# GpSimd in place of VectorE for the sums of the down weights' half slabs, two units ahead

## The chip, the cores and the metric

One core of a Trainium2 chip runs the whole program in one launch. The metric is the device time of that core in microseconds, the median of several executions; lower is better. A core has five instruction engines that run side by side and meet through semaphores: TensorE (PE; its weight loads are listed as PEld), VectorE (DVE), ScalarE (ACT), GpSimd (POOL) and SyncE (SP), which here only issues DMAs. ScalarE issues DMAs too.

## What is computed

A transformer-like trunk of two layers over 1088 tokens in fp32. Each layer is a mixer (sparse attention and a short convolution) and then a squared-ReLU MLP; the change lies in the last product of the MLP, `w_down`, 4096 x 1024 per layer:

```python
def trunk_layer(x, ..., w_up, w_down, topk):
    a, k_new, v_new, ki_new, conv_new = token_mixers(rms_norm(x, gains[0]), ...)
    x = x + rms_norm(a, gains[1])
    f = jnp.square(jax.nn.relu(rms_norm(x, gains[2]) @ w_up)) @ w_down
    x = x + rms_norm(f, gains[3])
    return x, k_new, v_new, ki_new, conv_new
```

## The kernel before

Every fp32 operand of a product is held as two fp32r numbers, a high part and a rest (value minus high part), and a product is three matmuls: high x high, high x rest, rest x high.

**The down projection by seven products.** The first 1024 rows of `w_down` are multiplied plainly, at the end (L778). The other 3072 rows are cut in two halves, and so are the 1024 output columns and the tokens, which gives 2x2 blocks; a scheme of Strassen's kind makes the product from seven block products ("forms", counted q = 0 to 6 in the order of `POSF = [0, 3, 1, 4, 2, 5, 6]`). A form has four pairs of output tiles, each in two **units**: eight units per form, `NUNIT` = 56 per layer, n = 8q + j. A unit is a half slab of weights, 128x768, six row blocks by 128 columns; TensorE makes 36 matmuls from it (`down_unit`, L1238).

**How a unit's weights come.** SyncE loads the half slab into `DR[n % 4]` (L567; buffers named DR or RAW in the profile), and for forms 1 and 3 a second one into `SK[n % 8]` (L566). For the units in `SUMMED` (forms 1, 3, 4 and 5; 32 per layer) the weights of the form are a sum or difference of two half slabs: `unit_add` on VectorE writes it into SK or DR (L2701, L2703). ScalarE then copies the high part into `DW[n % 4]` (`unit_high`; its copies are all on L1311), after TensorE has finished unit n - 4, and GpSimd makes the rest (L731). When GpSimd has made the rest of unit n (`unit_lo`), SyncE may load unit n + 4 into the buffer. TensorE waits for `unit_lo` before each unit.

**How a form's activations come.** ScalarE loads twelve blocks of 128x536 (128x528 in the second layer) of the next form into FL in three DMAs of 1.07 MB (L1832), copies their high parts into FB, and VectorE makes the rests (`form_low`, L2710), three at each of j = 4 to 7. TensorE waits for the first six before unit 0 of the form and for all twelve before unit 1. The products of a pair are added from PSUM to X by VectorE (`quads_out`, L2737, one to three instructions; L2739 copies for form 0), in the same in-order queue, behind the rests:

```python
for n in range(NUNIT):                      # VectorE
    q, j = divmod(n, 8)
    if n + 4 in SUMMED:
        unit_add(n + 4)
    if j >= 4:
        if q + 1 < len(POSF):
            form_low(q + 1, range(3 * (j - 4), 3 * (j - 3)))
    ...
    if j % 2:
        quads_out(q, j // 2)
```

Every engine works its list in the order in which it is written; nothing else sets the order. GpSimd's list in this stage is the 56 rests (L728 to L731), between the forms of the up weights (L695 to L716) and the splits of the plain down slabs (L600, L602).

Of the kernel before, what the change touches and what calls it, by code (L numbers as in the profile page):

```python
# [21 lines left out]
ALU, ACT, AX = mybir.AluOpType, mybir.ActivationFunctionType, mybir.AxisListType  # L22
# [67 lines left out]
POSF = [0, 3, 1, 4, 2, 5, 6]  # L90
NUNIT = len(POSF) * DPAIRS * 2
# [6 lines left out]
SUMMED = [n for n in range(NUNIT) if POSF[n // 8] in (2, 3, 4, 5)]  # L98
# [36 lines left out]
def key_tiles(t):  # L135

    if t == SPECIAL:
        return [(0, SEQ, MS, SPECIAL), (MS, PAST0, PAST, SPECIAL + 1)]
    return [(N_META + P * j, P * j, P, j) for j in range(t + 1)] + [(0, META0, N_META, SPECIAL)]
# [65 lines left out]
def build(nc, d):  # L205
    ctx = ExitStack()
    with ctx:
        names = set()

        def sem(name):  # L210
            assert name not in names
            names.add(name)
            return ctx.enter_context(nc.semaphore(name))
# [16 lines left out]
        def at(name, shape, dt, offset):  # L230
            return nc.alloc_sbuf_tensor_at(name, shape, dt, offset=offset)
# [66 lines left out]
        def prob(PA, i, g):  # L298
# [55 lines left out]
        DR = [RAW[:, 0, 0:UCOLS], RAW[:, 1, 0:UCOLS], at("DR2", [P, UCOLS], F32, r_q + 2 * ROW)[:, :],  # L354
              at("DR3", [P, UCOLS], F32, r_w + 4 * UCOLS * 4)[:, :]]
# [100 lines left out]
        unit_in = [sem("unit_in%d" % i) for i in range(4)]  # L456
        unit_sum, unit_hi, unit_lo, unit_done = sem("unit_sum"), sem("unit_hi"), sem("unit_lo"), sem("unit_done")
# [28 lines left out]
        def unit_loads(l, n):  # L486

            f, s = POSF[n // 8], n % 4
            before = sum(1 + (POSF[m // 8] in KEPT_OF) for m in range(n % 4, NUNIT, 4))
            return (l * before + sum(1 + (POSF[m // 8] in KEPT_OF) for m in range(s, n + 1, 4))) * 16  # L490

        def unit_value(l, n):

            return AREA[l][UNIT_SK][n % 8][:, :] if POSF[n // 8] in (2, 3, 4) else DR[n % 4]

        def sums_to(l, n):

            return l * len(SUMMED) + SUMMED.index(n) + 1
# [4 lines left out]
        def rows_at(u):  # L503

            a, kv, kt = STEPS[u]
            n = len(key_tiles(ORDER[a]))
            return [(j, g) for j, g in ROW_UNITS if j == NKV * a + kv + 2 and min(max(g, 0), n - 1) == kt]


        ENDS = [u + 1 for u, (_, _, kt) in enumerate(STEPS) if u + 1 == NU or STEPS[u + 1][2] == 0]  # L510

        def raw_q(l, k):
# [80 lines left out]
        def _(g_):  # L593
# [30 lines left out]
            for l in range(DEPTH):  # L624
# [63 lines left out]
                def forms(g, first=False):  # L688

                    n = l * NSTR + g  # L690
                    i = (l * (NRAW // 2) + KT // 2 + (S_UP + NPLAIN) // 2 + g + 1) * 16

                    def lo(f, value, done):
                        g_.wait_ge(form_hi, n * NPROD + f + 1)
                        g_.tensor_tensor(WF[f][:, 1, :, :], value, WF[f][:, 0, :, :].bitcast(F32), ALU.subtract)\  # L695
                          .then_inc(done, 1)

                    g_.wait_ge(raw_in[0], i)
                    g_.wait_ge(raw_in[1], i)
                    g_.tensor_tensor(S1F[:, :, :], a21, a22, ALU.add).then_inc(sum_made, 1)  # L700
                    lo(0, a11, form_made)
                    g_.wait_ge(sum_made, n * 4 + 1)
                    if first:
                        g_.wait_ge(slab_done, l * NDONE + D_MLP + NPLAIN)
                    else:
                        g_.wait_ge(prod_done, (n - 1) * NPROD + 3)
                    g_.tensor_tensor(WS[2][:, 1, :, :], S1F[:, :, :], a11, ALU.subtract).then_inc(sum_made, 1)
                    g_.wait_ge(sum_made, n * 4 + 2)
                    if first:
                        g_.wait_ge(t_step, l * 16 + 12)  # L710
                        g_.wait_ge(mid_stored, (l + 1) * NCH * 16)
                    g_.tensor_tensor(S4F[:, :, :], a12, WS[2][:, 1, :, :], ALU.subtract).then_inc(sum_made, 1)
                    lo(1, a12, form_made)
                    if not first:
                        g_.wait_ge(prod_done, (n - 1) * NPROD + 4)
                    g_.tensor_tensor(WS[3][:, 1, :, :], a21, a11, ALU.subtract).then_inc(sum_made, 1)  # L716
                    g_.wait_ge(sum_made, n * 4 + 3)
                    lo(2, WS[2][:, 1, :, :], form_made)
                    g_.wait_ge(sum_made, n * 4 + 4)
                    lo(3, WS[3][:, 1, :, :], raw_split)  # L720
                    lo(4, S1F[:, :, :], form_made)
                    lo(5, S4F[:, :, :], form_made)
                    lo(6, a22, raw_split)

                forms(0, True)
                with g_.Fori(1, NSTR) as g:
                    forms(g)
                for n in range(NUNIT):  # L728
                    hi, lo = (DW[n % 4][:, w, :, :].rearrange("p k n -> p (k n)") for w in range(2))
                    g_.wait_ge(unit_hi, l * NUNIT + n + 1)  # L730
                    g_.tensor_tensor(lo, unit_value(l, n), hi.bitcast(F32), ALU.subtract).then_inc(unit_lo, 1)  # L731
# [1299 lines left out]
        def _(dve):  # L2031
            V_ = nc.vector
# [129 lines left out]
            for l in range(DEPTH):  # L2162
# [215 lines left out]
                for b in range(BITS - 1, -1, -1):  # L2378
# [7 lines left out]
                    n = BITS - 1 - b  # L2386
# [107 lines left out]
                for u, (a, kv, kt) in enumerate(STEPS):  # L2494
                    i, n, rows = NKV * a + kv, len(key_tiles(ORDER[a])), rows_at(u)
# [19 lines left out]
                with dve.Fori(0, NMERGE // 2) as g:  # L2515
                    for s in range(2):
                        n = l * NMERGE + g * 2 + s
# [172 lines left out]
                products_out(NSTR - 1, False, True)  # L2690
                t_sums(NSTR - 1, 0, 4)

                def unit_add(n):

                    f, kept, raw_ = POSF[n // 8], SK[n % 8][:, :], DR[n % 4]
                    dve.wait_ge(unit_in[n % 4], unit_loads(l, n))
                    if f in (2, 5):
                        dve.wait_ge(unit_lo, l * NUNIT + n - 7)
                        dve.wait_ge(unit_sum, sums_to(l, n) - 8)
                    if f == 5:  # L2700
                        last = V_.tensor_tensor(raw_, raw_, kept, ALU.subtract)  # L2701
                    else:
                        last = V_.tensor_tensor(kept, kept, raw_, ALU.add if f == 4 else ALU.subtract)  # L2703
                    last.then_inc(unit_sum, 1)

                def form_low(q, kks):

                    for kk in kks:
                        dve.wait_ge(f_hi, (l * 7 + q) * NFORM + kk + 1)
                        V_.tensor_tensor(FB[q % 2][:, 1, kk, 0:2 * QWL[l]], FL[q % 2][:, kk, 0:2 * QWL[l]],  # L2710
                                         FB[q % 2][:, 0, kk, 0:2 * QWL[l]].bitcast(F32), ALU.subtract).then_inc(f_lo, 1)

                def a_low(j):

                    dve.wait_ge(a_hi, l * NPA + j + 1)
                    if j == 0 and TL[l] > 4 * QWL[l]:
                        V_.memset(A[:, :, :, 4 * QWL[l]:TL[l]].bitcast(F32), 0.0)
                    V_.tensor_tensor(A[:, 1, j, 0:4 * QWL[l]], ALO[:, j, 0:4 * QWL[l]],
                                     A[:, 0, j, 0:4 * QWL[l]].bitcast(F32), ALU.subtract).then_inc(a_lo, 1)
# [21 lines left out]

                for n in range(NUNIT):
                    q, j = divmod(n, 8)
                    if n + 4 in SUMMED:
                        unit_add(n + 4)
                    if j >= 4:
                        if q + 1 < len(POSF):
                            form_low(q + 1, range(3 * (j - 4), 3 * (j - 3)))
                        else:
                            a_low(2 * (j - 4))  # L2750
                            a_low(2 * (j - 4) + 1)
                    if j % 2:
                        quads_out(q, j // 2)
# [147 lines left out]
```

## Time and profile before

| | us |
|---|---|
| median of 3 runs | 3215.02 (3215.01 to 3217.68) |
| profiled execution, its own time | 3214.36 |
| its span, first to last instruction | 3212.4 |
| TensorE busy | 3070.5 (96%) |
| VectorE busy | 2170.1 (68%) |
| GpSimd busy | 1244.4 (39%) |
| ScalarE busy | 1064.3 (33%) |

Times in the trace count from the first instruction of the span. The seven products run from 1260 to 1518 us in the first layer and from 2842 to 3097 us in the second. A group of instructions is named by its line, engine and operation, then output tile <- input tiles. What stands in brackets at the end of a row of the timeline is how long the engine was idle before it and what released it.

### The profile page before, as it was taken

To read this page: it belongs to the slowest core of one execution; us is meant where nothing else is said; L and a number is where in the kernel's file an instruction comes from. 1 tells how busy PE (TensorE), PEld (TensorE's weight loads), DVE (VectorE), ACT (ScalarE), POOL (GpSimd) and SP (SyncE) were. 2 spreads that over 40 slices of the span, in tenths; PEclk is the share of its full clock that TensorE was granted. 3 is DMA by queue.
4 is the path that set the end of the run, shared out by engine and by line. 5 is a ranking of instruction groups with operands and counts; after the bars stand their busy time and mean duration, and the time that the engine had idled before them with its cause. 6 is when DMAs were issued, how large, how long until landed. Compare 5 with 4: busy or idle time off the path is not lost.

```text
span 3212.4 us, 54404 instructions
## 1 busy us (share of the span) xinstructions
PE 3070.5 (96%) x20484; PEld 2941.8 (92%) x20484; DVE 2170.1 (68%) x3821; ACT 1064.3 (33%) x1938; POOL 1244.4 (39%) x733
## 2 busy tenths in 40 slices
PE   5999999999999999999979999989999899999997
PEld 4989998679999999999979899977799899999997
DVE  6269998945585555675482799988456855576735
ACT  5430112750353333333244201137313433333321
POOL 2023333004637665445330333320154476644460
PEclk8999998999999999999999999989999999999998
DMA  3121223103323446654331212230132334466433
GB/s 136 54 72 46 68 87 134 34 28 128 115 82 121 146 136 214 238 191 171 99 120 60 67 47 80 91 115 27 67 107 96 109 127 147 147 247 241 170 127 108
DMA packets 164542, 369.50 MB, mean 115 GB/s; under 512 B 18496, under 2 KB 60064, under 8 KB 164384
## 3 DMA queue, kind: packets, MB, share of 16 engines
q10 hardware_dynamic: 114112, 209.45, 18.1%
q1 hardware_dynamic: 50272, 157.96, 15.2%
q8 instruction: 97, 1.59, 0.2%
q14 instruction: 61, 0.50, 0.0%
HBM read 261.53 MB, written 105.83 MB: 114 GB/s over the span
## 4 chain that ended last, share of the span: by engine, by line
PE 80%; DVE 10%; DMA 3%; issue 2%; ACT 2%; POOL 1%; ACTq 1%; DVEq 0%; SPq 0%; POOLq 0%
PE PS L769 26%; PE PS L1173 17%; PE PS L1238 13%; PE PS L778 8%; PE PS L852 5%; PE PS L1071 3%; PE PS L1031 2%; PE PS L1054 2%; PE PS L940 1%; PE PS L902 1%; PE PS L884 1%; DVE FB L2710 1%; DVE X L2139 1%; DVE X L2145 1%; DVE HN L2094 1%
## 5 line engine op out<-in xcount | busy, mean ns | idle before, releaser
L769 PE MATMUL PS<-H,W 128*128 128x358 f32 (+1 forms) x4032 | 662.0, 326 | 3.2 <-ACT SQ L1735 3.2
L769 PEld LDWEIGHTS PS<-H,W 128*128 128x128 f32 x4032 | 660.7, 189 | 3.3 <-issue 3.3
L600 POOL TENSOR_TENSOR W<-RAW,ones 128x1024 fp32r<-128x1024 f32 x80 | 157.4, 1967 | 880.6 <-PE PS L769 828.4
L1238 PE MATMUL PS<-FB,DW 128*128 128x268 f32 (+1 forms) x3456 | 428.1, 287 | 9.5 <-DVE FB L2710 9.5
L1238 PEld LDWEIGHTS PS<-FB,DW 128*128 128x128 f32 x3456 | 427.5, 190 | 9.8 <-POOL DW L731 9.8
L2363 DVE TENSOR_SCALAR_CACHE_REDUCE PASS<-SC,TC,CST 128x400 bf16<-128x400 f32 x372 | 356.1, 1020 | 1.7
L1173 PE MATMUL PS<-TT,WF 128*128 128x268 f32 (+1 forms) x2688 | 339.1, 285 | 0.8 <-POOL WF L695 0.8
L1173 PEld LDWEIGHTS PS<-TT,WF 128*128 128x128 f32 x2688 | 333.8, 188 | 1.0 <-POOL WF L695 1.0
L1173 PE MATMUL PS<-H,WF 128*128 128x268 f32 (+1 forms) x2016 | 260.2, 287 | 4.9 <-POOL WF L695 4.9
L1173 PEld LDWEIGHTS PS<-H,WF 128*128 128x128 f32 x2016 | 254.2, 190 | 5.3 <-POOL WF L695 5.3
L852 PE MATMUL PS<-WQ,H 128*128 128x364 f32 (+1 forms) x1296 | 239.9, 341 | 12.1 <-POOL WQ L607 5.5
L852 PEld LDWEIGHTS PS<-WQ,H 128*128 128x128 f32 (+1 forms) x1296 | 215.6, 187 | 21.6 <-ACT H L1311 8.9
L602 POOL TENSOR_TENSOR W<-RAW,W 128x1024 fp32r<-128x1024 f32 x80 | 211.4, 2642 | 6.3
L769 PE MATMUL PS<-A,W 128*128 128x358 f32 (+1 forms) x1152 | 188.7, 326 | 0.0
L769 PEld LDWEIGHTS PS<-A,W 128*128 128x128 f32 x1152 | 188.1, 189 | 0.6 <-issue 0.6
L778 PE MATMUL PS<-H,WR 128*128 128x358 f32 (+1 forms) x1008 | 167.1, 326 | 0.0
L778 PE MATMUL PS<-A,WD 128*128 128x358 f32 (+1 forms) x1008 | 166.9, 326 | 0.0
L778 PEld LDWEIGHTS PS<-A,WD 128*128 128x128 f32 x1008 | 164.0, 188 | 0.0
L778 PEld LDWEIGHTS PS<-H,WR 128*128 128x128 f32 x1008 | 163.6, 188 | 0.0
L1071 PE MATMUL PS<-PT,V 128*128 128x512 f32 (+2 forms) x304 | 157.6, 601 | 1.6 <-ACT PT L1311 1.6
L1031 PE MATMUL PS<-KS,QS 128*128 128x512 f32 (+6 forms) x480 | 134.9, 400 | 19.9 <-DVE LEAST L2427 17.1
L2737 DVE TENSOR_TENSOR X<-X,PS 128x536 f32<-128x536 f32 (+1 forms) x80 | 53.7, 703 | 147.1 <-PE PS L1238 147.1
(254 smaller groups left out, 4957.9 us busy)
## 6 DMA issues: line engine op xcount, KB each, us to landing
RAW<-in_w_slab SPq DMA_DIRECT2D x168, 512.0 KB, 3.6
RAW<-in_w_half SPq DMA_DIRECT2D x56, 384.0 KB, 4.3
DR<-in_w_half SPq DMA_DIRECT2D x56, 384.0 KB, 3.6
FL<-f_keep ACTq DMA_DIRECT2D x18, 1072.0 KB, 10.3
FL<-f_keep ACTq DMA_DIRECT2D x18, 1056.0 KB, 9.5
f_keep<-TB ACTq DMA_DIRECT2D x48, 268.0 KB, 4.5
f_keep<-TB ACTq DMA_DIRECT2D x48, 264.0 KB, 4.4
SK<-in_w_half SPq DMA_DIRECT2D x32, 384.0 KB, 3.8
```

The source lines that it names most:

```text
L600: g_.tensor_tensor(hi, raw, one, ALU.mult).then_inc(hi_split, 1)
L602: g_.tensor_tensor(lo, raw, hi.bitcast(F32), ALU.subtract).then_inc(raw_split, 1)
L769: mm = nc.tensor.matmul(PS[:, b0 + c, 0:cw], W[:, s, w, k, :], act[:, a, k, c * cw:(c + 1) * cw], start=(first and w == 0 and a == 0), sto ...
L778: mm = nc.tensor.matmul(PS[:, bank_, 0:cw], w[:, h, k, :], act[:, a, k, c * cw:(c + 1) * cw], start=(k == first and h == 0 and a == 0), st ...
L852: return nc.tensor.matmul(PS[0:m, b, 0:QG], H[:, a, k, t * P:t * P + m], WQ[:, k, w, b * QG:(b + 1) * QG], start=(k == 0 and w == 0 and a ...
L1031: last = nc.tensor.matmul(flat[0:m, c0 + dst:c0 + dst + w], QS[:, a % 3, GROUP * kv + q, 0:m], KS[:, 2 * kv + x, key:key + w], start=(x == ...
L1054: last = nc.tensor.transpose(PS[0:w, 4 + u % 2, g * m:(g + 1) * m], prob(PA, i, g)[0:m, dst:dst + w], cst["ident"][0:m, 0:m])
L1071: nc.tensor.matmul(PS[:, 6 + kv, 0:GROUP * m], V[0:w, vt, :], PT[0:w, u % 3, 0:GROUP * m], start=(kt == 0), stop=(kt == len(key_tiles(t)) ...
L1173: last = nc.tensor.matmul(PS[:, 2 * (f % 4) + c, 0:qw], WF[f][:, w, k, :], act(a, k, c * qw, (c + 1) * qw), start=(k == 0 and w == 0 and a ...
L1238: last = nc.tensor.matmul(PS[:, to + c, 0:qw], DW[s][:, w, kk - u * UNITK, :], down_act(q, a, kk, c * qw, (c + 1) * qw), start=(kk == 0 an ...
L2363: did(V_.tensor_scalar(PASS[0:m, SC_OFF[t]:SC_OFF[t] + EXT[t]], row(t), at_least, cst["negk"][0:m, c:c + 1], op, ALU.add, accum_out=CNT[0: ...
L2737: last = V_.tensor_tensor(to, to, of, ALU.add)
```

## The change

`unit_add` moves from VectorE to GpSimd, word for word but for the engine that issues it. On VectorE it ran at step n for unit n + 4; on GpSimd it runs at step n for unit n + 2, ahead of the rest of unit n. Its waits stay: for the loads of its unit (`unit_in`), and in forms 4 and 5 for the rest of the unit eight before it and the add eight before it. ScalarE, TensorE and SyncE wait for the same semaphores as before.

```diff
@@ GpSimd
                 with g_.Fori(1, NSTR) as g:
                     forms(g)
+                def unit_add(n):
+
+                    f, kept, raw_ = POSF[n // 8], SK[n % 8][:, :], DR[n % 4]
+                    g_.wait_ge(unit_in[n % 4], unit_loads(l, n))
+                    if f in (2, 5):
+                        g_.wait_ge(unit_lo, l * NUNIT + n - 7)
+                        g_.wait_ge(unit_sum, sums_to(l, n) - 8)
+                    if f == 5:
+                        last = g_.tensor_tensor(raw_, raw_, kept, ALU.subtract)
+                    else:
+                        last = g_.tensor_tensor(kept, kept, raw_, ALU.add if f == 4 else ALU.subtract)
+                    last.then_inc(unit_sum, 1)
+
                 for n in range(NUNIT):
+                    if n + 2 in SUMMED:
+                        unit_add(n + 2)
                     hi, lo = (DW[n % 4][:, w, :, :].rearrange("p k n -> p (k n)") for w in range(2))
                     g_.wait_ge(unit_hi, l * NUNIT + n + 1)
                     g_.tensor_tensor(lo, unit_value(l, n), hi.bitcast(F32), ALU.subtract).then_inc(unit_lo, 1)
@@ VectorE
-                def unit_add(n):
...
                 for n in range(NUNIT):
                     q, j = divmod(n, 8)
-                    if n + 4 in SUMMED:
-                        unit_add(n + 4)
                     if j >= 4:
```

GpSimd in the first layer, from the rest of unit 4 to that of unit 9. DW is where the rest goes, SK and DR or RAW are the half slabs. Before:

```order
L731 TENSOR_TENSOR DW_149<-RAW,DW_149 128x768
L731 TENSOR_TENSOR DW_150<-RAW,DW_150 128x768
L731 TENSOR_TENSOR DW_151<-DR_176,DW_151 128x768
L731 TENSOR_TENSOR DW_152<-DR_177,DW_152 128x768
L731 TENSOR_TENSOR DW_149<-SK_0_81,DW_149 128x768
L731 TENSOR_TENSOR DW_150<-SK_0_82,DW_150 128x768
```

The same place on GpSimd in the changed kernel, where L738 is the add and L746 the rest:

```order
L746 TENSOR_TENSOR DW_149<-RAW,DW_149 128x768
L746 TENSOR_TENSOR DW_150<-RAW,DW_150 128x768
L738 TENSOR_TENSOR SK_0_81<-SK_0_81,RAW 128x768
L746 TENSOR_TENSOR DW_151<-DR_176,DW_151 128x768
L738 TENSOR_TENSOR SK_0_82<-SK_0_82,RAW 128x768
L746 TENSOR_TENSOR DW_152<-DR_177,DW_152 128x768
L738 TENSOR_TENSOR SK_0_83<-SK_0_83,DR_176 128x768
L746 TENSOR_TENSOR DW_149<-SK_0_81,DW_149 128x768
L738 TENSOR_TENSOR SK_0_84<-SK_0_84,DR_177 128x768
L746 TENSOR_TENSOR DW_150<-SK_0_82,DW_150 128x768
```

The adds of units 8 and 9 now stand ahead of the rests of units 6 and 7, and so on, one add before each rest.

VectorE in the first layer, second half of form 2, where it makes the rests of form 3 (FB) between the X adds. Before:

```order
L2703 TENSOR_TENSOR SK_0_81<-SK_0_81,RAW 128x768
L2710 TENSOR_TENSOR FB_0_78<-FL_0_80,FB_0_78 128x536 x3
L2703 TENSOR_TENSOR SK_0_82<-SK_0_82,RAW 128x768
L2710 TENSOR_TENSOR FB_0_78<-FL_0_80,FB_0_78 128x536 x3
L2737 TENSOR_TENSOR X<-X,PS 128x536
L2703 TENSOR_TENSOR SK_0_83<-SK_0_83,DR_176 128x768
L2710 TENSOR_TENSOR FB_0_78<-FL_0_80,FB_0_78 128x536 x3
L2703 TENSOR_TENSOR SK_0_84<-SK_0_84,DR_177 128x768
L2710 TENSOR_TENSOR FB_0_78<-FL_0_80,FB_0_78 128x536 x3
```

The same place on VectorE in the changed kernel (L2712 the rests, L2739 the X adds):

```order
L2712 TENSOR_TENSOR FB_0_78<-FL_0_80,FB_0_78 128x536 x6
L2739 TENSOR_TENSOR X<-X,PS 128x536
L2712 TENSOR_TENSOR FB_0_78<-FL_0_80,FB_0_78 128x536 x6
```

The four adds are gone from between the rests; rests and X adds keep their order.

## Rows read from the trace of the kernel before

**Rows 1.** The page: the chain that ended last, by engine.
```profile
PE 80%; DVE 10%; DMA 3%; issue 2%; ACT 2%; POOL 1%; ACTq 1%; DVEq 0%; SPq 0%; POOLq 0%
```

**Rows 2.** Chain of waits, start us, us, what: first layer, then second.
```profile
1278.84 8.21 DMA RAW<-in_w_half
...
1287.07 0.96 DVE SK L2703
...
2868.78 0.96 DVE SK L2703
```

**Rows 3.** Stretches, engines' busy time; third number from the end: granted clock of TensorE.
```profile
1309.00:1311.00 2.00, 2.00 (x11) 2.00 (x10) 2.00 (x4) 0.40 (x1) 0.00 (x0) 0.50 1.05 419
2889.00:2891.00 2.00, 2.00 (x9) 2.00 (x10) 2.00 (x4) 0.00 (x0) 0.00 (x0) 0.50 1.04 395
1264.60:1266.10 1.50, 0.07 (x2) 0.04 (x1) 1.50 (x4) 0.84 (x1) 0.58 (x1) 1.00 1.02 405
```

**Rows 4.** Timeline of TensorE, cut at 1320 and at 2900 us.
```profile
1266.09 31.52 PE L1238 MATMUL PS<-H,DW 128*128 128x268 f32 x252 [1.44 <-DVE H L2623]
1307.36 12.80 PE L1238 MATMUL PS<-FB,DW 128*128 128x268 f32 x85 [5.29 <-DVE FB L2710]
...
2880.25 4.55 PE L1238 MATMUL PS<-FB,DW 128*128 128x264 f32 x36
2888.96 11.25 PE L1238 MATMUL PS<-FB,DW 128*128 128x264 f32 x78 [4.16 <-DVE FB L2710]
```

**Rows 5.** Groups (min/median/max ns), the half slabs' loads, VectorE's rests (mean ns last).
```profile
L2703 DVE TENSOR_TENSOR SK<-SK,RAW x12: 941/946/2393, 1287.1 to 1415.5; 128x768 f32<-128x768 f32 x12
...
L700 POOL TENSOR_TENSOR S1F<-RAW x28: 1283/1292/1301, 947.2 to 2807.2; 128x512 f32<-128x512 f32 x28
...
DMA to landing us min/median/max: 2.8/3.8/8.8
...
L2710 DVE TENSOR_TENSOR FB<-FL,FB 128x536 fp32r<-128x536 f32 x72 | 72.7, 1066 | 0.0
```

**Rows 6.** Timelines: GpSimd's rests near form 1, VectorE's copies; the long rest.
```profile
1276.60 3.65 POOL L731 TENSOR_TENSOR DW<-RAW,DW 128x768 fp32r<-128x768 f32 x2 [2.65 <-ACT DW L1311]
1280.21 1.85 POOL L731 TENSOR_TENSOR DW<-DR,DW 128x768 fp32r<-128x768 f32 x1
1288.99 1.99 POOL L731 TENSOR_TENSOR DW<-SK,DW 128x768 fp32r<-128x768 f32 x1 [4.38 <-ACT DW L1311]
...
1279.78 2.58 DVE L2739 COPY X<-PS 128x536 f32<-128x536 f32 x4 [3.17 <-PE PS L1238]
...
1443.99 4.70 POOL L731 TENSOR_TENSOR DW<-DR,DW 128x768 fp32r<-128x768 f32 x1 [2.62 <-ACT DW L1311]
```

**Rows 7.** Timeline of form 3, first layer: TensorE's releases, rests, X adds.
```profile
1394.12 1.34 DVE L2737 TENSOR_TENSOR X<-X,PS 128x536 f32<-128x536 f32 x2 [4.39 <-PE PS L1238]
1395.11 1.85 POOL L731 TENSOR_TENSOR DW<-SK,DW 128x768 fp32r<-128x768 f32 x1 [2.59 <-ACT DW L1311]
1398.63 0.85 ACT L1311 ACTIVATE DW<-SK 128x768 fp32r<-128x768 f32 x1 [1.98 <-PE PS L1238]
1403.98 1.32 DVE L2737 TENSOR_TENSOR X<-X,PS 128x536 f32<-128x536 f32 x2
1403.99 1.86 POOL L731 TENSOR_TENSOR DW<-SK,DW 128x768 fp32r<-128x768 f32 x1 [1.76 <-ACT DW L1311]
1409.33 3.61 DVE L2710 TENSOR_TENSOR FB<-FL,FB 128x536 fp32r<-128x536 f32 x3
1416.40 0.85 ACT L1311 ACTIVATE DW<-SK 128x768 fp32r<-128x768 f32 x1 [3.60 <-PE PS L1238]
1429.67 1.96 DVE L2737 TENSOR_TENSOR X<-X,PS 128x536 f32<-128x536 f32 x3 [4.38 <-PE PS L1238]
```

**Rows 8.** Timeline before the up projection, where VectorE and GpSimd both have work queued.
```profile
964.78 5.87 DVE L2576 TENSOR_TENSOR TT<-TF,TT 128x536 fp32r<-128x536 f32 x4
...
970.04 1.74 POOL L716 TENSOR_TENSOR WS<-RAW 128x512 f32<-128x512 f32 x1
```

More of the change, by code:

```diff
@@ L2691, in _ @@
                 t_sums(NSTR - 1, 0, 4)
-                def unit_add(n):
[L2695 to L2704, printed above, removed]
                 def form_low(q, kks):
```

## The prediction

> **What bounds the kernel now.** I read the page first. TensorE is busy for 96% of the span and is 80% of the chain that ended last [rows 1], so what only keeps it fed costs nothing. The down products (L1238) are one of its stretches: 3456 + 576 matmuls, and in them it waited in three places only: 5.3 us and 4.2 us for VectorE's rest of a form (FB, L2710), one per layer, and once 1.4 us [rows 4]. Between these waits it is the bound, and VectorE and GpSimd only have to be in time.
>
> The chain of waits says what the 5.3 us are made of [rows 2]: a half slab lands at 1287.07, and from there until TensorE goes on at 1307.36 VectorE alone is the path: add, three rests, add, three rests, copies, add, three rests, add, three rests. The adds are what the change takes off. After the wait TensorE runs at a granted clock of 0.50 (1.2 GHz) for a while [rows 3]: 85 matmuls take 12.80 us, where 252 take 31.52 (0.125 each, so 85 should take 10.6) [rows 4]. The stall costs 5.3 + 2.2 = 7.5 us; in the second layer 78 matmuls take 11.25 instead of 9.6, so 4.2 + 1.6 = 5.8 us. The 1.4 us wait left the clock at 1.00 [rows 3]. **13.3 us is all that can be won.**
>
> **What the change removes.** 64 adds of 128x768 from VectorE, 0.95 us each alone [rows 5]. Except at the two places above none is on the path.
>
> **What it adds.** The same 64 on GpSimd. The trace has no 128x768 add there, but it has the same form with 512 columns (1.29 us), and GpSimd's rest of 768 columns takes 1.85, or 3.65 for two in a row [rows 5, 6]. Adding and subtracting two SBUF tensors is one shape, so I take 1.83 in a row; the cheapest it could be is 1.29, the dearest 1.99. GpSimd then has 3.65 us in each unit of weights. A unit of TensorE is (1429.67 - 1394.12)/8 = 4.44 us, by VectorE's adds of the same pair in forms 3 and 4 [rows 7]. By itself that fits, with 0.8 us to spare.
>
> **What does not fit: the two engines exclude each other.** In the rows before 970 VectorE's TT rests and GpSimd's operations take turns, strictly one to one: four rests take 5.87 us, of which the first is free (0.70) and the others 1.72 each, and a GpSimd operation of 512 columns 1.74 in place of 1.29 [rows 8]. A turn of 1.72 holds 1.29 of GpSimd's, so each VectorE operation on two SBUF tensors costs GpSimd 0.43 us, and each GpSimd operation holds back one VectorE operation for all its length. Sums with a PSUM operand don't take part: two X adds took 1.32 us beside a GpSimd rest of 1.86 [rows 7]. With both queued, one pair takes 1.82 + 0.43 = 2.25 us, and GpSimd's two operations per unit make 4.5 us: just TensorE's pace of 4.44. GpSimd is then never idle long enough for a second VectorE operation, and **VectorE gets two rests per unit.** It needs twelve for each form.
>
> Now the deadline. VectorE's rests of form q+1 start after the X adds of pair 1 of form q (unit 4 begins) and the last six are wanted when unit 1 of form q+1 begins: five units, 22.2 us. In form 3 of the first layer: adds at 1394.12, last rest ended at 1409.33 + 3.61 = 1412.94, TensorE passed that point at 1416.40 (ScalarE's release for the unit three further on) [rows 7]. Slack 3.5 us, already with four adds and five waits for GpSimd in between.
>
> After the change, walked from these rows: the first rest is asked for at 1395.4, GpSimd's rest of 1395.11 is busy until 1396.96 [rows 7], so it ends at 1397.5. Then one per GpSimd operation, 2.25 us apart: add, rest, add, rest. Once, near 1399.6, GpSimd's rest has to wait for its high part (ScalarE starts that only when TensorE releases the buffer, at 1398.63 [rows 7]) and a second VectorE rest slips in for 0.7. The X adds in the middle (1.3 us) fall into one GpSimd operation. Last rest: 1397.5 + 0.7 + 10 x 2.25 = 1420.7. **TensorE waits 4.3 us.** While it waits GpSimd stops too, its buffers being full, but only two or three of its operations later. In form 2 (one X add per pair in place of two) the same walk gives 4.0 us, in form 4 (three) 4.5. Forms 1, 5 and 6 make their successors' rests when GpSimd has no adds to make: unchanged. In the second layer TensorE's unit is 0.05 us shorter, so 0.25 more each. Sum 2 x 12.8 + 0.75 = **26.4 us**. Waits of 5.3 and 4.2 us both brought the clock down for 2.2 and 1.6 us [rows 3, 4]; six times 2.0 is **12 us** (bounds: nothing, if the clock holds as after 1.4 us, and 13).
>
> **The start of form 1.** On GpSimd the add for unit 8 now stands ahead of the rest of unit 6 (listing in the section on the change), and it waits for the half slab that lands at 1287.07 (2868.8 in the second layer). The rest of unit 6 was made at 1280.21 [rows 6]; now add and rest end at 1290.8. TensorE wants it at 1266.09 + 5 x 4.50 = 1288.6 [rows 4]: a new wait of 2.3 us; in the second layer 2872.5 against 2880.25 - 2 x 4.39 = 2871.5, some 1.2. Queued behind it are the loads for units 10 and 11, which SyncE issues on the rests of 6 and 7; each lands some 4 us later (median 3.8 [rows 5]), when TensorE is at unit 8. VectorE instead makes its first six rests from 1282.4 on [rows 6], before any GpSimd add. The other six take turns with GpSimd, whose adds wait for loads: they end at 1293.2, 1295.5, 1297.8, 1300.0, 1302.3 and 1304.6, where TensorE, 2.3 us late, wants the last at 1304.4. So 7.5 becomes 2.6, and 5.8 becomes 1.7: 9.0 us won. Bounds: all of the 13.3; or nothing, if the clock also falls at the new wait and units 10 to 15, whose loads share the queue with 3.3 MB of forms and then took 8.2 us to land [rows 2], make TensorE wait 1 to 3 us more. I take **7 us** won.
>
> **Sum.** 26.4 + 12 - 7 = +31, which counts every pair as a loss. One slip of the turns is on record: VectorE made an add and three rests in a row while a GpSimd rest took 4.7 us [rows 6], and each such slip saves 2.2 us of a stall, or the stall's clock. I take 4 us off for them: +27 us on the profiled 3214.4, 3241.4. That run stands 0.7 under the median of 3215.0, so **3242 us**.
>
> **A rule of the Trainium skill.** The trace shows a VectorE operation costing GpSimd 0.43 us where it lasts 0.63 to 0.70 [rows 8]. The Trainium skill (SBUF — State Buffer, section "SBUF: two separate sides") calls the shared ports "an **exclusive lock**, not a bandwidth split", held for the whole instruction. The trace agrees on the exclusion but not on the whole length. By the page this change would end later than I say, so it is a rival.
>
> **Rivals.**
> (a) The turns cost full length. A pair is 1.84 + 0.70 = 2.54 us; the ten pairs of a walk add 10 x 0.29 = 2.9 us to each of six stalls, +17: 3259. Against it: four pairs at 1.72 in [rows 8].
> (b) GpSimd becomes the bound by its chain: rest n frees a buffer, the load takes 3.8 to 8.4 us, then add n+4, then rest. Two units per chain: 3.8 + 1.85 + 1.85 = 7.5 us against 8.9 is in time; with 8.4 us it is 12.1, 3.2 late, three or four times a layer where the forms' loads run. Its reserve of three units (13 us) covers that except at form 1. Some +20 on the forecast if the reserve is gone: 3262.
> (c) The starving is half as bad: one or two slips in each walk, stalls of 2.1 us, clock untouched: 6 x 2.1 - 7 = +6, 3221. The slip above speaks for it; in the other rows GpSimd gave way once at most.
> (d) The other side: VectorE is in time. It loses four adds (0.95 to 2.4 us each, 5.7 us in the walk of form 3 [rows 7]) against 3.5 us of slack that it has already; if GpSimd's added operations hold it back less than 9.2 us in a walk, no new stall appears, and the start of form 1 gives 9 to 13: 3205. It decides at about five extra waits of 1.8 us, and I count six or seven.
> (e) Nothing moves, because what is won at form 1 is lost in unit 6 and small stalls: with (c).
>
> **How the numbers follow.** Forecast 0.62 (3226 to 3258), (a) 0.10, (b) 0.08, (c, e) 0.10, (d) 0.10. The range from 3214 to 3262 leaves out (d) and the far part of (a) and (b). Within 0.2% (what a measurement can tell, 6.4 us) means 3208.6 to 3221.4: (c, e), 0.10; faster (d), 0.10; slower 0.80.
>
> **What would show it.** TensorE's waits in the down products: beside unit 6, waits of about 4 us for FB's rest at unit 1 of forms 3, 4 and 5, six in all, each followed by a clock of 0.50; VectorE's rests with a mean well over the 1.07 us of now [rows 5]; GpSimd's adds at 1.9 to 2.3 us. I am wrong if VectorE's rests for a form end before TensorE starts its unit 1, if GpSimd yields more than one turn at a time as a rule, or if TensorE's waits name GpSimd's DW.

## The result and the profile after

The changed kernel takes 3256.62 us (median of 4 runs, 3254.38 to 3261.48) against 3216.35 for the kernel before (3215.01 to 3221.0): ratio 1.0123, 95% interval 1.0111 to 1.0135. It is **40 us slower**; forecast were 27. The profiled execution is the slowest of the four (3261.48 us), so its trace has some 5 us more than the median.

The page of the changed kernel, busy time and the chain that ended last. GpSimd has 64 operations and 133 us more; VectorE has 64 fewer and no less busy time, because busy time counts what an instruction waits for its turn beside GpSimd (a rest of a form lasts 2.31 us in the median, where it lasted 0.70).

```profile
PE 3095.2 (95%) x20484; PEld 2963.3 (91%) x20484; DVE 2172.6 (67%) x3757; ACT 1064.2 (33%) x1938; POOL 1377.5 (42%) x797
...
PE 75%; DVE 13%; DMA 4%; issue 3%; ACT 2%; POOL 2%; ACTq 1%; SPq 0%; DVEq 0%; POOLq 0%
```

TensorE's waits in the changed kernel, 1240 to 1560 us, then 2850 to 3150 (total, times, longest). They answer to the waits in [rows 4].

```profile
PE PS L1253 <- DVE FB L2712: 14.2, 3, 5.7
PE PS L1253 <- POOL DW L746: 4.0, 3, 2.8
...
PE PS L1253 <- DVE FB L2712: 14.1, 4, 5.1
PE PS L1253 <- POOL DW L746: 4.0, 2, 2.2
```

The timeline of TensorE in the seven products of the first layer shows where they lie. The block that starts at 1299.70 is unit 8; 1316.45 is unit 11; 1384.08, 1427.12 and 1470.44 are unit 1 of forms 3, 4 and 5.

```profile
1265.48 24.10 PE L1253 MATMUL PS<-H,DW 128*128 128x268 f32 x180 [1.79 <-DVE H L2638]
1290.65 9.21 PE L1253 MATMUL PS<-H,DW 128*128 128x268 f32 x72 [1.06 <-POOL DW L746]
1299.70 4.62 PE L1253 MATMUL PS<-FB,DW 128*128 128x268 f32 x36
1304.53 9.17 PE L1253 MATMUL PS<-FB,DW 128*128 128x268 f32 x72 [0.21 <-POOL DW L746]
1316.45 64.01 PE L1253 MATMUL PS<-FB,DW 128*128 128x268 f32 x504 [2.76 <-POOL DW L746]
1384.08 37.31 PE L1253 MATMUL PS<-FB,DW 128*128 128x268 f32 x288 [3.62 <-DVE FB L2712]
1427.12 38.43 PE L1253 MATMUL PS<-FB,DW 128*128 128x268 f32 x288 [5.73 <-DVE FB L2712]
1470.44 68.43 PE L1253 MATMUL PS<-FB,DW 128*128 128x268 f32 x540 [4.88 <-DVE FB L2712]
```

In the second layer the same places wait for 1.79 (unit 6), 2.17 (unit 11), 3.86, 4.93 and 5.11 us. Behind each wait of over 2 us the granted clock is at half for a while, here in two-microsecond stretches after the waits at 1427 and 1470 (third number from the end); these answer to [rows 3].

```profile
1428.00:1430.00 2.00, 2.00 (x11) 2.00 (x11) 0.22 (x1) 0.00 (x0) 1.79 (x1) 0.50 1.05 403
1471.00:1473.00 2.00, 2.00 (x11) 2.00 (x11) 1.16 (x2) 0.00 (x0) 1.04 (x1) 0.50 1.05 398
```

The mechanism itself, in form 3 of the first layer, VectorE and then GpSimd. It answers to [rows 7]; L746 is the rest, L738 the sum.

```profile
1399.21 1.34 DVE L2739 TENSOR_TENSOR X<-X,PS 128x536 f32<-128x536 f32 x2 [7.56 <-PE PS L1253]
...
1414.58 12.39 DVE L2712 TENSOR_TENSOR FB<-FL,FB 128x536 fp32r<-128x536 f32 x6
1426.90 1.32 DVE L2739 TENSOR_TENSOR X<-X,PS 128x536 f32<-128x536 f32 x2
...
1415.09 2.31 POOL L746 TENSOR_TENSOR DW<-SK,DW 128x768 fp32r<-128x768 f32 x1
1417.36 2.31 POOL L738 TENSOR_TENSOR SK<-SK,RAW 128x768 f32<-128x768 f32 x1
1419.64 2.30 POOL L746 TENSOR_TENSOR DW<-SK,DW 128x768 fp32r<-128x768 f32 x1
1421.90 2.27 POOL L738 TENSOR_TENSOR SK<-SK,DR 128x768 f32<-128x768 f32 x1
```

What VectorE and GpSimd hold in turns, one operation at a time, is called the port from here on. GpSimd's operations start 2.28 us apart, 0.45 us more than the 1.83 that the same operation lasts alone, and six rests of VectorE take 12.39 us where 6 x 0.63 = 3.8 would do. The twelfth rest ends at 1414.58 + 12.39 = 1426.97; TensorE had finished unit 0 of form 4 at 1384.08 + 37.31 = 1421.39.

### The profile page after: what moved, and what is told of

Same layout as the page of the kernel before. It is cut to its first block, busy times and chain, and to the rows that moved or that the text cites. A ratio compares the mean times of both kernels' runs of the same rounds, so it can differ in the third digit from the quotient of the medians.

```text
span 3259.6 us, 54404 instructions
## 1 busy us (share of the span) xinstructions
PE 3095.2 (95%) x20484; PEld 2963.3 (91%) x20484; DVE 2172.6 (67%) x3757; ACT 1064.2 (33%) x1938; POOL 1377.5 (42%) x797
## 4 chain that ended last, share of the span: by engine, by line
PE 75%; DVE 13%; DMA 4%; issue 3%; ACT 2%; POOL 2%; ACTq 1%; SPq 0%; DVEq 0%; POOLq 0%
PE PS L784 26%; PE PS L1188 16%; PE PS L1253 9%; PE PS L793 8%; PE PS L867 5%; DVE FB L2712 4%; PE PS L1086 3%; PE PS L1046 2%; PE PS L1069 2%; PE PS L955 1%; PE PS L917 1%; DMA RAW<-in_w_half 1%; PE PS L899 1%; DVE X L2154 1%; DVE X L2160 1%
## 5 line engine op out<-in xcount | busy, mean ns | idle before, releaser
L1253 PE MATMUL PS<-FB,DW 128*128 128x268 f32 (+1 forms) x3456 | 442.5, 292 | 33.5 <-DVE FB L2712 28.3
L1253 PEld LDWEIGHTS PS<-FB,DW 128*128 128x128 f32 x3456 | 440.3, 195 | 35.4 <-issue 23.7
L2712 DVE TENSOR_TENSOR FB<-FL,FB 128x536 fp32r<-128x536 f32 (+1 forms) x144 | 231.8, 1674 | 0.0
L2739 DVE TENSOR_TENSOR X<-X,PS 128x536 f32<-128x536 f32 (+1 forms) x80 | 53.6, 702 | 184.4 <-PE PS L1253 184.4
```

The costliest lines, as they stand in the source:

```text
L1253: last = nc.tensor.matmul(PS[:, to + c, 0:qw], DW[s][:, w, kk - u * UNITK, :], down_act(q, a, kk, c * qw, (c + 1) * qw), start=(kk == 0 an ...
```

## The experiments

My theory was the forecast's: the rests of VectorE starve beside two GpSimd operations per unit. Rivals were that GpSimd's own chain is late, that the start of form 1 spoils what follows, and that it is the amount of work and not the taking of turns.

**1. Form 1 alone.** GpSimd makes the sums of form 1 only; the last two lines of the diff are VectorE's.

```diff
-                    if n + 2 in SUMMED:
+                    if n + 2 in SUMMED and (n + 2) // 8 in (1,):
                         unit_add(n + 2)
...
+                    if n + 4 in SUMMED and (n + 4) // 8 not in (1,):
+                        unit_add(n + 4)
```

> GpSimd makes only the sums of form 1 (units 8 to 15); those of forms 3, 4 and 5 are back on VectorE, four units ahead, as before the change. Theory (VectorE's rests starve because each has to take its turn behind one of two GpSimd operations per unit): no waits of 3.6 to 5.7 us at unit 1 of forms 3, 4, 5; the start of form 1 as in the changed kernel, waits of 1.1 and 2.8 us in the first layer, 1.8 and 2.2 in the second, in place of 5.3 and 4.2, so 0 to 6 us faster than before: 3211 to 3216. Rival (GpSimd's own chain of load, sum and rest is late, and VectorE's rests are only late because of it): about half of the loss stays, 3230 or more.

Measured: 3216.36 us, ratio 1.000 (0.9991 to 1.001). No form after the first makes TensorE wait for rests; what is left, by TensorE's waits in both layers, lies at the start of the products:

```profile
PE PS L1253 <- POOL DW L746: 6.1, 4, 2.5
PE PS L1253 <- DVE H L2638: 4.0, 3, 1.8
PE PS L1253 <- DVE X L2754: 2.7, 1, 2.7
```

So the start of form 1, where I had counted on 7 us, gains nothing that can be measured: waits for VectorE (5.3 and 4.2 us) have become waits for GpSimd, and once 2.7 us for a copy of products to X. The low clock is not gone either: it was 0.53 and 0.50 behind two of GpSimd's waits, of 2.3 and 2.5 us.

**2. Forms 3, 4 and 5 alone.** The same edit with `(3, 4, 5)` in place of `(1,)`.

> The other half alone: GpSimd makes the sums of forms 3, 4 and 5, VectorE those of form 1. Theory: all six waits for VectorE's rests stay at 3.6 to 5.7 us (28 in all) with some 12 us of low clock behind them, and the start of form 1 is as before with 5.3 and 4.2: 38 to 44 us slower than before. Rival (the loss comes out of form 1, which leaves GpSimd without reserve for the forms that follow): under 15 us slower.

Measured: 3257.67 us (one run), as slow as the whole change. TensorE's waits for VectorE's rests (eight: the two at form 1 and the six) are all there:

```profile
PE PS L1253 <- DVE FB L2725: 34.9, 8, 5.1
PE PS L1253 <- DVE H L2638: 3.6, 2, 1.8
```

The whole loss is in forms 3, 4 and 5, and form 1 has no part in it.

**3. Half as long.** The changed kernel with sums of half the columns; the kernel leaves out the other half, so its output is another.

```diff
-                        last = g_.tensor_tensor(raw_, raw_, kept, ALU.subtract)
+                        last = g_.tensor_tensor(raw_[:, 0:UCOLS // 2], raw_[:, 0:UCOLS // 2], kept[:, 0:UCOLS // 2], ALU.subtract)
```

(and the other line likewise).

> The changed kernel with sums over 384 of 768 columns; half of each sum is left out. As many turns as in the changed kernel, but every second one is about 0.9 us shorter. Theory: the mean turn falls from 2.28 to 1.83 us, twelve rests end 5 us earlier, and the six waits for them shrink from 3.6 to 5.7 us to under 1.5 us each: 3210 to 3222. Rival (what counts is that there are two waits for GpSimd per unit, semaphores and all, not their length): waits over 3 us stay, 3245 or more.

Measured: 3207.86 us (one run). TensorE waits for no rest of VectorE any more; in both layers together there are three waits for GpSimd of 2.2 us in all. The number of GpSimd's operations does no harm; their time on the port does. The time is even below the range that I gave, since at form 1 TensorE then waits 2.2 us in place of 9.5, with no low clock behind it: the two layers' products take 9.9 us less than in the kernel before, of the 13.3 that there were to win.

**4. Longer rests.** The changed kernel, VectorE's rests three blocks at a time.

```diff
-                    for kk in kks:
-                        dve.wait_ge(f_hi, (l * 7 + q) * NFORM + kk + 1)
-                        V_.tensor_tensor(FB[q % 2][:, 1, kk, 0:2 * QWL[l]], FL[q % 2][:, kk, 0:2 * QWL[l]],
-                                         FB[q % 2][:, 0, kk, 0:2 * QWL[l]].bitcast(F32), ALU.subtract).then_inc(f_lo, 1)
+                    k0, k1 = kks.start, kks.stop
+                    dve.wait_ge(f_hi, (l * 7 + q) * NFORM + k1)
+                    V_.tensor_tensor(FB[q % 2][:, 1, k0:k1, 0:2 * QWL[l]], FL[q % 2][:, k0:k1, 0:2 * QWL[l]],
+                                     FB[q % 2][:, 0, k0:k1, 0:2 * QWL[l]].bitcast(F32), ALU.subtract).then_inc(f_lo, k1 - k0)
```

> The changed kernel, but VectorE makes the rests of a form three blocks at a time: 4 instructions of 128x1608 in place of 12 of 128x536, the same elements. Theory (turns, not elements, are short): 4 turns of at most 1.85 + 1.7 us, so no wait for a form's rests; waits at units 6 and 11 stay; 3205 to 3215, faster than before. Rival (the shared port is simply full, 37 us of work in 35.6 us per form): the work is the same, so waits of 2 us and more stay, or GpSimd is late in its place: 3235 or more.

Measured: 3241.13 us, ratio 1.0078 (1.0061 to 1.0095). Half right on both sides: the waits for VectorE are gone, as the theory said, but GpSimd is late in its place, 31 times, as the rival said. TensorE's waits, then GpSimd's own from 1290 to 1530 us:

```profile
PE PS L1253 <- POOL DW L746: 23.7, 31, 2.5
...
POOL SK L738 <- DMA RAW<-in_w_half: 25.5, 6, 7.0
```

GpSimd sat 25.5 us in the first layer waiting for half slabs. That points not at the port but at the chain rest, load, sum, rest; 5. and 6. test it.

**5. Sums one unit ahead.** The changed kernel with `if n + 1 in SUMMED: unit_add(n + 1)`: three rests, not two, stand between the one that lets a load start and the sum that needs it.

> The changed kernel with GpSimd's sums one unit ahead of its rests instead of two: the sum of unit 8 stands ahead of the rest of unit 7, not 6. Theory: the waits at units 6 and 11 (1.1 and 2.8 us, 1.8 and 2.2 us) go with their clock, the six waits for VectorE's rests stay as they are: 3245 to 3251. Rival (the distance sets how tight the turns are): the six waits change by over 1 us each.

Measured: 3259.39 us, ratio 1.013 (1.0114 to 1.0145). A miss: no gain. The waits at units 6 and 11 did go, but waits of 2.3 and 1.8 us for rests came at unit 9, and the six grew to 4.3, 6.4, 6.5, 4.5, 6.5 and 6.7 us. In all:

```profile
PE PS L1253 <- DVE FB L2712: 39.0, 8, 6.7
```

In the changed kernel GpSimd waited some 21 us for loads between 1290 and 1530 us, here 2.0. While it waited, VectorE had the port. That this is what the six waits grew by is argued from these numbers, not tested by itself.

**6. Both.** Sums one unit ahead, rests three blocks at a time.

> GpSimd's sums one unit ahead, and VectorE's rests three blocks at a time. With the long rests alone TensorE waited 23.7 us in 31 pieces for GpSimd. Theory A (with sums two units ahead a load that takes 4 to 8 us stands directly on the path of rest, load, sum, rest): with the load issued three steps ahead of its sum this goes, waits for GpSimd under 5 us, 3206 to 3214. Theory B (port full: sixteen operations of 1.82 us and four turns of 1.6 us make 35.5 us of a form's 35.6): waits for GpSimd of 10 to 20 us stay, 3222 to 3236.

Measured: 3207.69 us (10 runs, 3199.16 to 3216.70), ratio 0.9969 (0.9958 to 0.9981): faster than before. Against 4. the one unit less of lead gives 33 us. Theory A holds: TensorE doesn't wait for GpSimd at all in the products of this trace. So a port that is full by my estimate (16 operations of 1.82 and four turns of 1.6 us in 35.6) can be run if no load stands in the chain. The ten times are spread widely, and the trace has something that I did not expect. Timeline of VectorE, then of GpSimd, form 4 of the second layer:

```profile
3000.77 21.27 DVE L2712 TENSOR_TENSOR FB<-FL,FB 128x1584 fp32r<-128x1584 f32 x2
...
3000.79 1.83 POOL L736 TENSOR_TENSOR RAW<-RAW,SK 128x768 f32<-128x768 f32 x1
3002.59 1.84 POOL L746 TENSOR_TENSOR DW<-SK,DW 128x768 fp32r<-128x768 f32 x1
3004.39 1.84 POOL L736 TENSOR_TENSOR RAW<-RAW,SK 128x768 f32<-128x768 f32 x1
3006.20 1.83 POOL L746 TENSOR_TENSOR DW<-RAW,DW 128x768 fp32r<-128x768 f32 x1
...
3017.43 2.95 POOL L746 TENSOR_TENSOR DW<-DR,DW 128x768 fp32r<-128x768 f32 x1 [0.38 <-ACT DW L1326]
```

Two rests of 1.7 us each took 21 us: GpSimd made nine operations back to back, at 1.80 us distance, and VectorE had its turn only when GpSimd had to wait 0.38 us for ScalarE. TensorE waited 5.78 us for it.

**7. The same kernel again,** for a second trace.

> The same kernel as e7_lead1_merge3, for a second trace. In its first trace one long rest of VectorE stood for 17 us while nine GpSimd operations went by, and its ten times were spread over 17 us. If GpSimd's streak is chance, another trace has it elsewhere, or not at all, and a time between 3199 and 3217 that goes with it. If it belongs to the order of the instructions, it is again in form 4 of the second layer, with a wait of some 5.8 us.

Measured: 3204.70 us; the longest rest is 3.5 us, no streak anywhere, and the largest wait after form 0 is 0.5 us. So the order of the instructions alone does not bring the streak. That streaks are what spreads the ten times is likely, but two traces do not show it.

**8. Longer rests without the change.** The kernel before, with the edit of 4.

> The kernel before (sums on VectorE, four units ahead), with its rests made three blocks at a time: 4 instructions of 128x1608 per form in place of 12. Theory (a form's rests are a matter of turns): at the start of form 1 each group of three rests loses its one wait for GpSimd of 1.8 us, four groups, 7 us, more than the stalls of 5.3 and 4.2; both go, with their low clock: 13 us faster than before, 3201 to 3207. Rival (GpSimd, which now waits up to 1.6 us for each long rest, becomes late, as it did where it also made the sums): 3212 or more, with waits for GpSimd's DW.

Measured: 3206.20 us (3203.09 to 3208.11), ratio 0.9966 (0.9954 to 0.9978). **This beats both kernels**, with sums left on VectorE. Start of form 1, timeline of VectorE, to be read against [rows 2]:

```profile
1284.40 0.96 DVE L2703 TENSOR_TENSOR SK<-SK,RAW 128x768 f32<-128x768 f32 x1 [4.48 <-DMA RAW<-in_w_half]
1285.28 1.83 DVE L2710 TENSOR_TENSOR FB<-FL,FB 128x1608 fp32r<-128x1608 f32 x1
...
1298.92 1.82 DVE L2710 TENSOR_TENSOR FB<-FL,FB 128x1608 fp32r<-128x1608 f32 x1
```

Three rests take 1.83 us where they took 3.5 with GpSimd's rest between the second and the third. From the landed half slab to the last rest it is 16.3 us, not 20.1, and TensorE waits 1.26 and 0.25 us, not 5.3 and 4.2. The gain at form 1 is had with 24 rests per layer in place of 72, and nothing moved to another engine.

**9. Form 1's rests alone.** As 8., with the long rests only for q = 1.

> The kernel before, with only form 1's rests made three blocks at a time. Theory (what the long rests win on VectorE is the start of form 1 and nothing else): as fast as with all forms' rests long, 3202 to 3208. Rival (they also free something elsewhere): over 3211.

Measured: 3206.55 us, ratio 0.9966 (0.9955 to 0.9978). All of it comes from the start of form 1.

**10. Rests cut in two.** The changed kernel, each rest as two instructions of 268 columns.

> The changed kernel with each of VectorE's rests cut into two instructions of 268 columns: the same elements in 24 instructions per form, not 12. Theory (turns): one half rest per GpSimd operation, so about ten of 24 are made by the time TensorE wants all; then three more turns, and the rest without GpSimd at 0.35 us each: waits of 8 to 11 us in place of 3.6 to 5.7, 3280 to 3300. Rival (the amount of VectorE's work): under 3 us more than the changed kernel per wait, 3257 to 3270.

Measured: 3268.52 us (one run), in the rival's range. A miss for the theory as I had put it. VectorE, form 3 of the first layer:

```profile
1403.10 17.26 DVE L2714 TENSOR_TENSOR FB<-FL,FB 128x268 fp32r<-128x268 f32 x12
...
1421.52 9.90 DVE L2714 TENSOR_TENSOR FB<-FL,FB 128x268 fp32r<-128x268 f32 x12
```

Twelve half rests, six blocks, take 17.3 and then 9.9 us, the second time beside a GpSimd that was idle for 3 us of it; whole rests took 13.0 and 12.4 us for six. At one half rest for each GpSimd operation of 2.03 us the first twelve would have taken some 24 us. Short operations cost GpSimd less per turn (most of its operations ran 2.03 us, not 2.31), so GpSimd has gaps of its own while TensorE sets the pace (0.3 to 0.8 us before each rest), in which further half rests can be made. So the count of turns does not say how late VectorE is; for the changed kernel the time on the port does. TensorE's unit is 4.44 us, GpSimd's two operations hold 3.65 of it, 0.8 is left; a whole rest needs 0.45, so VectorE gets 1.8 rests per unit and twelve take 6.8 units, where five are to be had. That sum says without a walk that VectorE must be late; how late also hangs on GpSimd, which stops soon after TensorE does. But the sum takes GpSimd as never giving way. By it the long rests of 6. (four of 1.6 us, eight units) would be late in every form too, and but for the streak they made TensorE wait once, for 1.05 us: a long instruction that has its turn holds GpSimd back, which has a reserve to give. Both the time on the port and the length of VectorE's instructions count. Half of VectorE's elements in as many instructions, which would part the two further, was not measured.

## Why the prediction was right, point by point

- **The six waits for rests.** Forecast 4.0, 4.3, 4.5 and 0.25 more in the second layer, 26.4 us; measured 3.6, 5.7, 4.9, 3.9, 4.9, 5.1, together 28.1. Shown by 2. to be the whole loss. Within them the walk of form 3 was 1.2 us short (last rest 27.8 us after the X adds, not 26.6): the one extra rest that I let slip in did not come there. That the sum of the six is so close is in part luck, since the misses have both signs (0.4 less, 1.4 and 0.4 more in the first layer). A turn is 2.28 us, forecast 2.25.
- **The clock behind them.** Forecast 12 us. Full speed is (211.14 - 0.3 - 2.2)/1692 = 0.1233 us per matmul in the first layer of the kernel before (its block of 1692 matmuls after the 5.3 us wait); 288 matmuls should take 35.8 and took 38.43 and 37.31, 540 should take 66.9 and took 68.43. With the second layer's blocks worked out alike it is 1.5, 2.6, 1.5, 2.6, 1.7 and 2.8 us, 12.7 in all.
- **The start of form 1** is the term that was mis-sized: 9.0 us won by the sum, 7 taken, 2 measured. The waits at unit 6 were right in kind (1.1 and 1.8 us, forecast 2.3 and 1.2). Left out of the sum, and only in its bound and in rival (b), were the waits at unit 11: 2.76 and 2.17 us and 1.6 and 1.5 of clock. The chain of waits of the changed kernel shows their cause, a load that took 7.9 us to land beside the forms' loads, the sum of unit 13 behind it, and the rest of unit 11 behind that on GpSimd:

```profile
1304.50 0.33 SPq L566
...
1304.87 7.89 DMA RAW<-in_w_half
...
1312.82 1.82 POOL SK L738
1314.64 1.77 POOL DW L746
...
1316.45 3.56 PE PS L1253 x16
```

- **Slips of the turns:** 4 us were taken off for them; none of note came in this trace. This was wrong twice over, since 6. shows that a slip can also go against VectorE.
- **The waits of the kernel before.** The prediction counts three waits in the seven products; there were four. The second layer's form 0 waits 1.78 us too, and behind that wait the clock was at 0.50 (timeline of TensorE, then a stretch, granted clock third from the end). So that waits under 2 us leave the clock alone was not to be read from this trace:

```profile
2847.58 32.83 PE L1238 MATMUL PS<-H,DW 128*128 128x264 f32 x252 [1.78 <-DVE H L2623]
...
2848.00:2850.00 2.00, 2.00 (x11) 2.00 (x10) 1.87 (x2) 0.00 (x0) 1.12 (x1) 0.50 0.11 42
```

- **The sum:** 27 + 1.7 (waits) + 0.7 (clock) + 5 (form 1) + 4 (slips) = 38. Another 1.6 us of low clock stands behind the 1.79 us wait in form 0, which the kernel before went through at full clock in its first layer. That makes 40, as far apart as the medians are; but the terms come from two profiled executions that are 47.1 us apart, so the agreement with 40 is in part luck. In those two the seven products take 43.7 us more. The terms leave out 3 us of it, by my estimate the tail of a block (the 0.3 us above) at each of ten more stops. The other 3.4 us lie outside the seven products, and no run says why.
- **Rival (a),** turns of full length, is out: 0.45 us per rest, not 0.70. The section "SBUF: two separate sides" of the Trainium skill's page SBUF — State Buffer, which says that the loser blocks for the whole instruction, agrees with GpSimd holding VectorE for all of its 1.83 us and not with VectorE costing GpSimd 0.45 of its 0.63 to 0.70.
- **Rival (b)** shows in the changed kernel only at the start of form 1, in the waits at unit 11 (4.9 us, and 3.1 of clock), not as the 20 us that it named; but it was the next bound: in 4., where the rests were no longer in the way, it cost 24 us.
- **Rival (d),** VectorE in time, needed the sums to hold VectorE back by under 9.2 us in a walk. 3. comes near that case, and the gain at form 1 was then real.

## What to carry over

Moving work from VectorE to GpSimd did not relieve VectorE here, where both work on SBUF tensors: count the time on the port (a GpSimd sum here 1.83 us where VectorE's was 0.95), and ask which of the two has the shorter reserve before its deadline, since that one starves. When an in-order engine is slowed by another's turns, try longer instructions first: fewer, larger operations won 10 us here with nothing moved. And on an engine that sets loads free, a sum that waits for such a load belongs as late in the list as its consumer allows: one unit later was worth 33 us in 6., though nothing in 5., where another wait stood in front.

## What was not expected of the hardware

- VectorE and GpSimd do not always take turns one to one. Mostly they alternate, but in one trace GpSimd took nine operations in a row (16 us) over a waiting VectorE, until it had to wait itself, and in the kernel before VectorE took an add and three rests in a row over a waiting GpSimd. Two traces of one kernel differed in it; its ten times spread over 17 us where the kernel with long rests on VectorE alone spread over 5. What decides it stays open.
- Waits of 1.4 to 1.8 us sometimes bring the clock to half and sometimes don't: after 1.44 us (kernel before, first layer) it stayed at 1.00, after 1.79 us at the same place in the changed kernel it was 0.50, and after 1.73 us in the kernel of 8. it stayed at 1.00. Every wait of 2.2 us or more in the changed kernel cost 1.5 to 2.8 us of low clock, but in 1. the clock stayed at 1.00 behind a wait of 2.73 us. So the length of the wait alone does not decide it, and what does stays open.
